# Linear attention: one step's gated output products moved behind the next values' low halves and gate product on VectorE, with a third place for the gate

## What is computed

```
scores  = causal(q_dec @ k_inv^T)                  # per chunk of 64 tokens, per head
o       = scores @ v + q_dec @ state               # state: sum over the chunks before
state   = decay * state + (k * exp(G_last - G))^T @ v
o_gla   = o * rsqrt(mean(o*o) + eps) * norm_w * silu(gate)
```

## Time and profile before

| | us |
|---|---|
| median of 3 runs | 833.5 (833.31 to 833.54) |
| span of the profiled execution | 831.5 |
| TensorE busy | 817.2 (98%) |
| VectorE busy | 587.1 (71%) |
| ScalarE busy | 437.4 (53%) |
| POOL busy | 83.5 (10%) |
| mean granted TensorE clock | 0.998 of full speed |

### The profile page before, as it was taken

The page is one execution under the profiler, slowest core; times in us unless marked ns, Lnnn a source line. Parts: engine busy times, 40 slices in busy tenths (PEclk is TensorE's granted clock), DMA queues, the critical chain, the costliest instruction groups (busy, mean ns, idle before and its releaser), DMA issues.

```text
span 831.5 us, 13218 instructions
## 1 busy us (share of the span) xinstructions
PE 817.2 (98%) x4586; PEld 683.9 (82%) x4586; DVE 587.1 (71%) x1362; ACT 437.4 (53%) x1057; POOL 83.5 (10%) x123
## 2 busy tenths in 40 slices
PE   8999999999999999999999999999999999999997
PEld 7887888888788888878888898888888888888885
DVE  6788668767578667767857877599845563367997
ACT  7865445444345445445545666543655464356543
POOL 3100122210000111111100000000010000001201
PEclk9999999999999999999999999999999999999999
DMA  8321359962143245655512158855331111206945
GB/s 296 106 82 39 111 169 193 182 132 71 33 136 109 82 75 98 125 95 121 108 61 83 58 187 248 279 155 142 126 103 56 60 62 40 89 13 133 214 97 202
DMA packets 70409, 99.21 MB, mean 119 GB/s; under 512 B 6596, under 2 KB 38472, under 8 KB 70344
## 3 DMA queue, kind: packets, MB, share of 16 engines
q1 hardware_dynamic: 52360, 64.29, 24.2%
q0 software_dynamic: 15392, 29.36, 19.7%
q10 hardware_dynamic: 2592, 4.72, 1.7%
HBM read 83.68 MB, written 31.46 MB: 138 GB/s over the span
## 4 chain that ended last, share of the span: by engine, by line
PE 95%; DVE 3%; issue 1%; ACT 1%; DMA 0%; POOL 0%; ACTq 0%; DVEq 0%
PE bank L1843 14%; PE bank L1845 14%; PE bank L1844 14%; PE banks2to L1843 10%; PE banks2to L1845 10%; PE banks2to L1844 10%; PE banks6to L1915 5%; PE banks2to L2102 4%; PE bank L2128 3%; PE banks2to L2038 1%; PE bank L2130 1%; PE banks6to L2062 1%; PE banks6to L1845 1%; PE banks6to L1843 1%; PE banks6to L1844 1%; DVE neg_max L1642 1%
## 5 line engine op out<-in xcount | busy, mean ns | idle before, releaser
L1845 PE MATMUL bank<-w_hi,actT_lo 128*128 128x512 f32 x412 | 161.2, 391 | 0.0
L1843 PE MATMUL bank<-w_hi,actT_hi 128*128 128x512 f32 x384 | 154.7, 403 | 0.1
L1844 PE MATMUL bank<-w_lo,actT_hi 128*128 128x512 f32 x384 | 149.6, 390 | 0.0
L1380 DVE SCALAR_TENSOR_TENSOR w_lo<-w_raw,vecs,w_hi 128x512 fp32r<-128x512 f32 x120 | 86.8, 749 | 43.4 <-ACT w_hi L1098 43.4
L1845 PEld LDWEIGHTS bank<-w_hi,actT_lo 128*128 128x128 f32 x412 | 77.3, 188 | 16.8
L1098 ACT ACTIVATE w_hi<-w_raw,vecs 128x512 fp32r<-128x512 f32 x120 | 82.4, 718 | 7.4 <-DMA w_raw<-in_w_ckv 4.4
L1843 PEld LDWEIGHTS bank<-w_hi,actT_hi 128*128 128x128 f32 x384 | 73.0, 190 | 15.0 <-DVE w_lo L1380 1.4
L1844 PEld LDWEIGHTS bank<-w_lo,actT_hi 128*128 128x128 f32 x384 | 72.3, 188 | 13.3
L984 POOL TENSOR_TENSOR rs_o<-var_o,neg_half 128x1 f32<-128x1 f32 (+1 forms) x48 | 28.8, 600 | 380.2 <-DVE var_o L1669 258.3
L1845 PE MATMUL banks2to<-w_hi,actT_lo 128*128 128x512 f32 x164 | 64.0, 390 | 0.0
L1263 ACT ACTIVATE prob<-banks2to,neg_maxs 128x128 f32<-128x128 f32 (+7 forms) x64 | 46.9, 740 | 13.5 <-DVE neg_maxs L1643 13.2
(11 more groups left out here) (368 smaller groups left out, 2048.8 us busy)
## 6 DMA issues: line engine op xcount, KB each, us to landing
w_raw<-in_w_in SPq DMA_DIRECT2D x56, 256.0 KB, 3.2
out_sums<-in_w_out POOLq DMA_DIRECT2D x11, 1024.0 KB, 9.4
late_sums<-in_w_co POOLq DMA_DIRECT2D x11, 1024.0 KB, 9.2
w_raw<-in_w_ckv SPq DMA_DIRECT2D x32, 256.0 KB, 3.5
w_raw<-in_w_cq SPq DMA_DIRECT2D x32, 256.0 KB, 2.8
stage_in<-in_x SPq DMA_DIRECT2D x8, 512.0 KB, 4.5
tile_a<-mixed ACTq DMA_DIRECT2D x16, 256.0 KB, 3.3
x_res<-in_x SPq DMA_DIRECT2D x8, 512.0 KB, 6.5
```

Of the source, the lines that this page charges most:

```text
L1380: return dve.scalar_tensor_tensor(dst, src, scale, hi.bitcast(F32), ALU.mult, ALU.subtract)
L1843: pe.matmul(dst, l_hi, r_hi, start=start, stop=False)
L1844: pe.matmul(dst, l_hi, r_lo, start=False, stop=False)
L1845: return pe.matmul(dst, l_lo, r_hi, start=False, stop=stop)
```

## The change

Four edits. The stage `ofin` s-1 moves from ahead of `proj` s+1 to behind `gmul` s+1, still ahead of `o` s (not in the last step). The gate gets a third place, `gate3`, in the second half of `qk_tok`, and the places go round by (s + 1) % 3. `gmul` s waits for `ofin` of one step further back. ScalarE's copy for the second differential projection, the first to write that half of `qk_tok`, waits until the `ofin` of step 13 is done.

```diff
         passed = [("ofin", s - 1)] if s else []
         if s + 1 < GLA_STEPS:
-            plan.extend([*passed, ("proj", s + 1), ("gmul", s + 1), ("o", s)])
+            plan.extend([("proj", s + 1), ("gmul", s + 1), *passed, ("o", s)])
         else:
             plan.extend([*passed, ("proj", s + 1), ("o", s)])
...
+        gate3 = qk_tok[:, 1, :, :].rearrange("p j c -> p (j c)")
...
+        def gla_gate(s):
+
+            return gate3 if (s + 1) % 3 == 2 else gate[:, 256 * ((s + 1) % 3):256 * ((s + 1) % 3) + 256]
...
                     wait(act, tq_pe, i - 1)
+                    if i == 1:
+                        act.wait_ge(of_dve, GLA_STEPS - 2)
                     copy(qk_tok[:, i % 2, :, ROPE:DQK],
...
-                    wait(dve, of_dve, s - 1)
-
-                    dve.scalar_tensor_tensor(gate[:, 256 * (s % 2):256 * (s % 2) + 256], tanh_g[:, :], 1.0,
+                    wait(dve, of_dve, s - 2)
+                    dve.scalar_tensor_tensor(gla_gate(s), tanh_g[:, :], 1.0,
                                              bank0[:, 256:512], ALU.add, ALU.mult).then_inc(pj_dve, 1)
...
-                        last = dve.scalar_tensor_tensor(mix_out[:, c], o_f[:, j, hh, :],
-                                                        rs_o[:, j, hh:hh + 1], gate[:, c], ALU.mult, ALU.mult)
+                        last = dve.scalar_tensor_tensor(mix_out[:, c], o_f[:, j, hh, :], rs_o[:, j, hh:hh + 1],
+                                                        gla_gate(s)[:, cols(hh)], ALU.mult, ALU.mult)
```

## The result

| | before | changed |
|---|---|---|
| median, 21 runs each | 833.57 (833.31 to 834.54) | 834.80 (834.41 to 835.18) |
| span of the profiled execution | 831.5 | 833.4 |

The account below looks back on a forecast made before the run. TensorE, busy 98%, was taken as the bound, paced by V and, in steps with a tile, by the loop over R. 1.08 - 0.27 + 0.26 + 0.10 = +1.17 us gave 834.7 us, range 833.2 to 835.9.

Parts of the forecast that it names:

- V: VectorE's instruction making the values' low halves; said to set TensorE's pace, with `kv` starting 0.52 to 0.53 us behind it.
- R: VectorE's reduction of the output sums; in steps with a weight tile the loop closes over it, 7.87 us.
- (1): VectorE: no work added or removed; `ofin` (0.52 us) only moves from ahead of V to behind the gate product.
- (2): VectorE's loop from V to R and back: 7.87 us in both orders, so no gain in steady state.
- (3): ScalarE, nine steps with a tile: the values' copy now waits for ke_hi; loop 0.12 us longer each, +1.08 in all.
- p: Time ke_hi keeps ScalarE to itself before the values' copy can start; taken as 0.16 to 0.17 us.
- the rival that saw no overlap for such a source: Copy starts only at the end of ke_hi, which reads PSUM: loop 8.07, +1.9 us, 835.4 us; chance 0.23.
- (4): Step 2: the first `ofin` leaves its place ahead of V, which comes earlier once: -0.27 us.
- (5): Late st_lo delays TensorE's output products behind three-tile steps: +0.26 from step 14, +0.10 from step 6; ordinary steps nothing.
- (6): The third gate place, the changed waits, SP's store and POOL's queue: claimed to cost nothing.
- One sign of being wrong: TensorE waiting at the output products for longer than at `kv`; it would mean (5) is the cost.
- everything behind 205 us shifted by one number: Sign of being right: behind the linear-attention steps, all work moves by the same time.

Follow-up runs that it names:

- run 4: Changed kernel with the gated products behind the reduction of the output sums, ahead of the weight tile: 830.96 us, ratio 0.9972.
- run 3: Kernel before, with ScalarE's ke_hi of the next step moved up behind sc_hi: 833.37 us, ratio 0.9999.
- run 2: Changed kernel with ScalarE's ke_hi of the next step moved up into its idle time behind sc_hi: 833.64 us, ratio 1.0002.
- run 8: The changed kernel measured and profiled once more, with no further edit: 834.82 us, ratio 1.0017.
- run 5: Changed kernel with the gated products behind the reduction of the output sums only in steps 6 and 14: 834.17 us, ratio 1.0007.
- run 1: Changed kernel with the gated products put back ahead of the values' low halves; third gate place and waits stay: 833.52 us, ratio 1.0001.
- run 6: Against run 4: VectorE's order is V, R, gate product, gated products; V waits only for ScalarE's values copy, tanh for V: 836.04 us, ratio 1.0031.
- run 7: Changed kernel with the gated products behind both the reduction of the output sums and the weight tile's w_lo: 834.12 us, ratio 1.0009.

## Why the prediction was right, point by point

- **What bounds (V sets the pace, and R sets V in steps with a tile).** Right. Run 4 breaks the chain over R and gets 7.58 to 7.63 in all steps; run 3 shows that ScalarE did not bind before.
- **(1), (2) VectorE's own loop gives nothing.** Right. In run 2, where ScalarE is out of the way, the changed order takes 7.86 to 7.87.
- **(3) ScalarE's chain, 0.12 a step with p at 0.16 to 0.17.** The mechanism is right and shown by run 2. p measured 0.16, the loop 7.98 and not 7.99, so the nine steps paid 0.11 each, about 1.0 against the 1.08 forecast. ke_hi, which reads PSUM, overlapped with the copy behind it by 0.26 - 0.16 = 0.10 us. The Trainium skill's 93 ns ("ScalarE: Activation LUTs", "What ACT_TABLE_LOAD costs") agrees with it, and the rival that saw no overlap for such a source is wrong.
- **(4) Step 2.** -0.27 forecast, -0.24 to -0.26 measured over the three profiles of this order (the first, runs 2 and 8).
- **(5) Steps 14 and 6.** Step 15 was 0.26 by forecast and 0.37 by the trace: a wait of 0.30, and 0.07 more within the output products, which the forecast had not counted. For step 6, the +0.10 was mis-sized: "V of step 8 waits for TensorE and hides most of it" is wrong. V of step 8 could hide no more than 0.08 us of it, because `kv` of that step already stood that close behind the scores; +0.21 was measured. Together the two are 0.58 where 0.36 was forecast, and run 5 gave back 0.65 of time for them (0.56 by the shifts). For the ordinary steps the conclusion held but not the reason as it was put. The 0.14 us wait at the output products is there, and run 2 shows that it costs nothing. But `kv` does not wait "longer after": the distance from the last scores to `kv` fell from 0.43 to 0.31, since the late output products (0.14 and another 0.08 within them) used up more than the 0.11 by which the step grew. 0.20 us of cover was left.
- **(6) The gate place, waits and queues.** Right: run 1.
- **The sum.** 1.0 - 0.25 + 0.37 + 0.21 = 1.33 by the trace, as the shift behind step 15 has it (1.3 from step 1 on), against 1.17 forecast. Both terms of (5) were too small, that of (3) was too large by 0.1, and the medians differ by 1.23. That the total is within 0.1 is therefore in part luck; the range would have held without it.
- **The signs named ahead.** One sign of being wrong was seen: TensorE waited at the output products for longer than at `kv`, 4.6 us in all against 2.4, and about 0.39 against 0.15 us in a step with a tile. The conclusion tied to it, "then (5) is the cost", does not follow. In run 2 the waits at the output products are as long (4.5 us in all), and the nine steps are back at 7.86 to 7.87. Which of two waits is longer does not tell which one sets the pace; that is told by what the last one follows, and `kv` followed V by 0.52 to 0.53 us in all steps but step 8. Of the signs of being right all were seen but one: "everything behind 205 us shifted by one number" held up to 514 us and then not, for a reason (the transfer shown under run 8) that has nothing to do with the change.

What stays open: what run 6 lost at step 8 and behind step 15 is read from its trace and was not tested, and why the output products take 0.07 to 0.08 us longer behind a wait was not looked into.

## What to carry to other kernels

When an engine idles ahead of the instruction that others wait for, look whether the engine's work forms a loop from step to step. Inside such a loop an instruction costs the same in front of the urgent one as behind it; only a place where the engine waits for another makes it free (run 4, at 2.5 us), and the moved work must stand ahead of the instruction that waits, not behind it (run 7). Then count what moves later in the same round: here ScalarE, whose way from R to V was 0.41 us shorter than VectorE's (5.95 + 0.16 + 0.69 = 6.80 against 7.21), was 0.11 longer once VectorE's was cut by 0.52. And the time at which a bank comes free is as much an output of a step as the value that is computed from it (run 6).

## What the runs showed of the hardware that was not expected

- Landing of weight tiles around 513 to 520 us varies from run to run enough to stall TensorE by 0 to 0.6 us, in kernels whose order of work is the same there (5.88 us from issue to landing in the longest shown). The difference of two profiled spans can so stand off the difference of the medians by half of a small effect (1.9 against 1.2). The shift of one fixed instruction before that place was good to about 0.1 us: it drifted by 0.06 and 0.08 from step 1 to step 15 in runs 1 and 3, where nothing should move, and by 0.13 between two profiles of the changed kernel.
- Apart from that, the chain of waits repeated to 0.01 or 0.02 us a step in the profiles with one order of work. That is why effects of 0.1 us a step could be told from single profiles, and why the sum of hand-over times worked at this size.
